# A two-layer hybrid trunk on one core: cached keys and values over four places, output blocks reordered, low weights in four pieces

## The chip, the core and the metric

The kernel runs on one core of one Trainium2 chip. The metric is device microseconds from start to end of one execution, the median of several. TensorE (PE) does the matrix products, VectorE (DVE) and ScalarE (ACT) take results out of PSUM, GpSimd (POOL) works from SBUF to SBUF, and SyncE (SP) issues most of the DMAs. Each engine works through its own list of instructions in order; semaphores are all that ties the lists together.

## The reference, cut to what matters

A prompt (1 x 1024 tokens) and a sample group (8 sequences of 4 tokens, 8192 past positions each) go through the same two layers with model width 1024. Layer 0 is a convolution module beside a dilated sliding-window attention, layer 1 a short gated convolution beside a chunked spatial gate; behind each mixer comes a SwiGLU of 2816. All is float32.

```python
def _dilated_attn_sample(q, k_ext, v_ext, d, rel_bias_table, grp):
    idx = Wb + np.arange(S)[:, None] - steps[None, :] * d      # 129 positions, stride 1, 4 or 16
    s = jnp.einsum('nshd,nskhd->nhsk', q, k_ext[:, idx_c]) * (Dh ** -0.5) + bias
    lse = jax.nn.logsumexp(s, axis=-1)
    o = jnp.einsum('nhsk,nskhd->nshd', jnp.exp(s - lse[..., None]), v_ext[:, idx_c])
...
out = jnp.concatenate([a, attn], axis=-1) @ P['e_w_out'][e]    # a: 256 channels, attn: 256
x = x + mod[:, 2] * out
h = _rmsnorm(x, P['norm_ffn_g'][layer]) * (1 + mod[:, 4]) + mod[:, 3]
gu = h @ P['ffn_w_gate_up'][layer]
```

For each of the 8 sequences the sample attention reads the keys and the values of its three groups from the caches, 9 tiles of 128 rows of 256 floats: 1152 KB for one set of keys, the same for one set of values.

## The kernel before

**Order.** `make_plan` writes one list of items (`Item`), and every engine's block walks through that list and emits its own part of each item. What stands earlier in the list is earlier on every engine. `mixed` and `among` spread one list of items evenly among another. SyncE alone walks through a list shifted by `ahead`: the stores of the prompt's keys and values of a group (`store_tokens`) come 16 items after their place.

**Dense products.** Weights come in units of 1 MB: SyncE loads a unit into one of three slots (`w_raw`), ScalarE rounds it to a high half (`split_hi`, L1061), and GpSimd subtracts to get the low half, in the place of the raw weights (`split_lo`, L2106). A product is high x high, high x low and low x high. PE waits on `w_lo_done`. A unit's split is emitted with the item of the unit before it. Results go to two PSUM places of three banks in turn (`big`); VectorE or ScalarE frees one (`big_free`) before PE writes it again.

**Around the sample attention.** The attention of the prompt's third group (`attention(2)`: scores, transpose, values, store, 16 steps) is mixed with the sample group's keys. For each sequence `b` five pieces of keys are transposed (`s_kt`, L2664; VectorE evacuates the even ones, ScalarE the odd ones), and three score products (`s_qk`, L2675) use them with `q_own`, which VectorE builds in the item `sample_in` (L1955, L1956). In the same stretch `ln_mid` (L1399, L1574) makes the two halves of the convolution's output, whose place on VectorE is free when the prompt's stores (`k_stored`) have landed. The keys lie in `cache`, two places; `load_cache` (L947 to L949) loads a set into a place when the set before it there has been used (`last_keys`), three DMAs each.

After the scores come the softmax (`s_soft`), the first unit of the output projection (`down_a`, eight blocks of 128 rows, `down_part`; VectorE evacuates each, L1567), the transposed weights `pT` (`s_pt`, L1409 on ScalarE, L1989 to L1993 on VectorE), the values (`s_pv`, L2712, 9 products a set) in pairs, each followed by `s_rows` and a block. Four blocks come before `s_pt`, four after the pairs. The values have three places. `comb` (L2000 to L2020) mixes the prompt's three groups on VectorE; `s_out`, `combine` and `mid_lo` (L2033) make the second half of the mixer's output, which `bound` needs: the last unit of the output projection with the next norm.

**Norm.** `bound` runs residual, norm and split in three turns of columns. For a turn VectorE makes `nt` (L1514), ScalarE `h_hi` (L1111, L1113, L1115), VectorE and GpSimd the even and odd `h_lo` (L1540, L2127), and PE takes products as they are made (`project_as_made`, L2342). Ahead of the third turn's lows GpSimd splits a unit: on GpSimd `lows(it, 1, ...)`, `split_lo(it.of.unit + 2)`, `lows(it, 2, ...)`. The third turn's VectorE part is `scaled_and_low(it, 2)`.

**Memory.** `cache` and the transposed keys lie where the first layer's `h_hi` was, `cache_v` over the transposed keys; `w_raw` slots 0 and 1 stand idle while the sample attention runs.

Of the kernel before, what the change touches and what calls it, by code (L numbers as in the profile page):

```python
# [172 lines left out]


# [6 lines left out]
def make_plan():  # L181
# [171 lines left out]
    mixed(last[:3], [])  # L353
    items.append(Item("sample_in"))
# [29 lines left out]
    def down_pieces(weights, col, **kw):  # L384

        made = []

        def piece(m):
            def place():
                if not made:  # L390
                    made.append(Item("down", weights=weights, col=col, unit=take("unit"), big=take("big", 8), **kw))
                items.append(Item("down_part", of=made[0], m=m, begins=m == 0, ends=m == KT - 1))
            return place

        return [piece(m) for m in range(KT)]

    down_a = down_pieces("e_w_out", 0, layer=0, gate=2, src="mid", slot=0, ready=1)
    for place in down_a[:4]:
        place()
# [12 lines left out]
    items.append(Item("combine", big=take("big", 2)))  # L412
    into_norm("e_w_out", 1, (0, 1), layer=0, gate=2, src="mid", slot=1, ready=2)
# [73 lines left out]
def build_trunk(nc: bass.Bass, A: dict, O: dict):  # L487
# [105 lines left out]
    cache_v = at("cache_v", R_HH + 18432, [P, 9, 256])  # L593
    o_sum = at("o_sum", R_V, [P, 4, 512])
# [46 lines left out]
    with ExitStack() as ctx:  # L641
# [70 lines left out]
        cache_loaded = [sem(f"cache_loaded{s}") for s in range(3)]  # L712
# [35 lines left out]
        for it in dense_items:  # L748
            unit_end[it.unit] = (big_ready, it.big + (2 + it.skip if it.kind == "project" else 8))
# [122 lines left out]
        def cached(c):  # L872

            slot = cache_at(c)[0]
            return cache_v if slot == 2 else cache[:, slot]
# [30 lines left out]
        def _(sp):  # L906
# [25 lines left out]
            def load_cache(c):  # L932

                kv, b = divmod(c, NB)
                if c == 0:
                    sp.wait_ge(big_ready, by_role["q", 2].big + 2)
                elif 2 <= c < NB + 2:
                    sp.wait_ge(misc_ready, last_keys[c - 2].misc + 1)
                elif c == NB + 2:
                    sp.wait_ge(big_ready, score_item.big + 1)  # L940
                elif c > NB + 2 and b % 2:
                    sp.wait_ge(v_used, (b - 3) // 2 + 1)
                elif c > NB + 2:
                    sp.wait_ge(misc_ready, values_of[b - 3].misc + 1)
                rows = [A[f"cache_b_kv{g}"][0, b, :, kv].rearrange("w h e -> w (h e)") for g in range(3)]
                to, loaded = cached(c), cache_loaded[cache_at(c)[0]]
                sp.dma_start(to[:, 0, :], rows[0]).then_inc(loaded, 16)  # L947
                sp.dma_start(to[:, 1:5, :], rows[1].rearrange("(j s) e -> j s e", s=4)).then_inc(loaded, 16)
                sp.dma_start(to[:, 5:9, :], rows[2].rearrange("(j s) e -> j s e", s=16)[:, 0:NS, :]).then_inc(loaded, 16)  # L949
# [46 lines left out]
            for it in ahead():  # L996
# [6 lines left out]
                elif it.kind == "tokens_store":  # L1003
                    store_tokens(it.of.g)
                elif it.kind == "ada":
                    order = ada_units.index(it)
                    if order < 2:
                        sp.wait_ge(x_loaded[(4, 7)[order]], 16)
                    elif order < 8:
                        raw_landed(ada_units[order - 2].raw)  # L1010
                    if it.raw.slot >= 4:
                        sp.wait_ge(x_turned, 2 * (it.raw.slot - 4) + 2)
                        sp.wait_ge(x_squared, 2 * (it.raw.slot - 4) + 2)
                    layer, cb = divmod(it.k, 24)
                    load_raw(it.raw, as_project, columns(A["ada_w"][layer], cb))
                elif it.kind in ("project", "down") or it.begins:
                    load_unit((it.of or it).unit + 1)
                elif it.kind == "sample_in":
                    load_cache(0)
                    load_cache(1)  # L1020
                elif it.kind == "s_kt" and it.c == 4:
                    load_cache(it.b + 2)
                elif it.kind == "s_soft":
                    load_cache(NB + 2)
                elif it.kind == "s_pv" and it.b + 3 < NB:
                    load_cache(NB + it.b + 3)
# [27 lines left out]
        def _(act):  # L1054
# [170 lines left out]
            for it in plan:  # L1225
# [102 lines left out]
                elif it.kind == "down_part":  # L1328
                    if it.begins and it.of.unit + 1 in unit_end:
# [762 lines left out]
        def _(pool):  # L2092
# [9 lines left out]
            def split_lo(u):  # L2102
# [3 lines left out]
                pool.tensor_tensor(w_lo[raw_of[u].slot], w_raw[raw_of[u].slot], w_hi[u % 2].bitcast(F32), ALU.subtract)\  # L2106
                    .then_inc(w_lo_done, 1)
                splits[0] = u + 1
# [28 lines left out]
            for it in plan:  # L2137
# [47 lines left out]
                elif it.kind == "bound":  # L2185
                    if it.of.unit + 1 in unit_end:
                        split_lo(it.of.unit + 1)
                    if it.role == "norm":
# [4 lines left out]
                        split_lo(it.of.unit + 2)  # L2193
                        lows(it, 2, (1, 3, 5, 7))
# [9 lines left out]
                elif it.kind == "down_part":  # L2204
                    if it.begins and it.of.unit + 1 in unit_end:
# [64 lines left out]
        def _(pe):  # L2270
# [22 lines left out]
            def project(u, t):  # L2293
                pe.wait_ge(w_lo_done, u + 1)
# [4 lines left out]
            def project_part(it, m, k):  # L2299

                if m == 0 and k == 0:
                    pe.wait_ge(w_lo_done, it.unit + 1)
# [3 lines left out]
            def first_products(it):  # L2306
# [3 lines left out]
                if it.which == "high":  # L2310
                    if it.k == 0:
                        pe.wait_ge(w_lo_done, u + 1)
# [20 lines left out]
            def project_as_made(u, t, it):  # L2333

                n = it.n
                pe.wait_ge(w_lo_done, u + 1)
# [37 lines left out]
            def down_blocks(it, x_hi, x_lo):  # L2374

                u, t = it.of.unit, it.of.big
                pe.wait_ge(w_lo_done, u + 1)
# [54 lines left out]
            def down(u, t, x_hi, x_lo, only=None):  # L2432
                if only in (None, 0):
                    pe.wait_ge(w_lo_done, u + 1)
# [12 lines left out]
            for it in plan:  # L2447
# [211 lines left out]
                elif it.kind == "s_kt":  # L2659
# [3 lines left out]
                    for j, (tile, a) in enumerate(KEY_PARTS[it.c]):  # L2663
                        mm = pe.transpose(misc(it.misc)[:, j * P:j * P + P], cached(it.b)[:, tile, a * P:a * P + P], ident)  # L2664
# [38 lines left out]
                elif it.kind == "s_pv":  # L2703
# [7 lines left out]
                    for t in range(9):  # L2711
                        mm = pe.matmul(misc(it.misc)[32 * (t % 4):32 * (t % 4) + 32, 256 * (b % 2):256 * (b % 2) + 256],  # L2712
                                       pT[:, t, b // 2:P:4],
                                       cached(c)[:, t, :], start=(t < 4), stop=(t >= 5), skip_group_check=True)
# [96 lines left out]
```

## Time and profile before

| | |
|---|---|
| median of 3 runs | 2604.43 us (2603.75 to 2606.38) |
| the profiled execution | 2611.14 us, its span 2609.3 us |
| TensorE busy | 2513.5 us (96%), mean granted clock 0.985 |
| VectorE, ScalarE, GpSimd busy | 914.0 (35%), 585.7 (22%), 510.6 us (20%) |
| chain that ended last | PE 73%, DVE 3%, ACT 2%, DMA 1%, issue 1% |
| `w_lo` on GpSimd | 93 instructions, 4639 ns mean |
| HBM | 228.04 MB read, 62.54 MB written, 111 GB/s over the span |

Two different executions stand in the table: the runs are timed without a profile, the span and all rows come from one profiled execution. Times in rows are microseconds from the start of its span. A row of the timeline has start, length, engine, line, operation, output and inputs with their shapes and a count; in brackets is how long the engine stood idle before it and what ended that. `q` behind an engine's name is its sequencer, which issues a DMA. An engine that is idle but not on the chain costs nothing.

### The profile page before, as it was taken

Reading aid. Unit: us, or ns where it says so; the run is one execution under the profiler, and the core shown is the slowest. Engines: PE = TensorE matmul, PEld = TensorE weight load, DVE = VectorE, ACT = ScalarE, POOL = GpSimd, SP = SyncE. Lnnn points to the kernel's source line nnn. Section 1 sums busy time; section 2 is a strip of 40 time slices with the busy share of each in tenths; the row PEclk is TensorE's granted clock in tenths of the full one; section 3 lists DMA queues with packets and bytes.
Section 4 is the critical chain, followed back from the end, with each engine's and each line's share of the span. In section 5 each row is a group of like instructions: output and inputs, shape, how many; then the busy total and the mean of one; then the engine's idle time right before and its main releaser. Section 6 shows DMA issues by size and latency. Waiting matters only on the chain.

```text
span 2609.3 us, 36572 instructions
## 1 busy us (share of the span) xinstructions
PE 2513.5 (96%) x16279; PEld 2393.7 (92%) x16279; DVE 914.0 (35%) x1679; ACT 585.7 (22%) x901; POOL 510.6 (20%) x209
## 2 busy tenths in 40 slices
PE   7999899889999999999999999999999999999998
PEld 6987778568999999999999899988999999999998
DVE  4366552556022222211224512546122222222226
ACT  5112223415111111111112411144211111111113
POOL 3210010103211221211211322122212221122210
PEclk8999999999999999999999999999999999999999
DMA  9322322770221222221221579311101111011101
GB/s 314 141 63 89 120 87 76 266 246 17 81 81 50 96 81 65 81 97 49 82 97 49 185 269 302 106 34 33 49 33 49 49 49 49 33 49 49 49 33 67
DMA packets 163963, 249.10 MB, mean 95 GB/s; under 512 B 6164, under 2 KB 150825, under 8 KB 162526
## 3 DMA queue, kind: packets, MB, share of 16 engines
q1 hardware_dynamic: 150762, 179.29, 20.9%
q0 software_dynamic: 4784, 63.31, 7.0%
q10 hardware_dynamic: 8260, 4.15, 0.6%
q8 instruction: 129, 2.11, 0.3%
q14 instruction: 28, 0.23, 0.0%
HBM read 228.04 MB, written 62.54 MB: 111 GB/s over the span
## 4 chain that ended last, share of the span: by engine, by line
PE 73%; DVE 3%; ACT 2%; DMA 1%; issue 1%; SPq 0%; ACTq 0%; DVEq 0%
PE ps L2286 66%; PE ps L2385 3%; PE ps L2520 1%; PE ps L2342 1%; DVE h_lo L1540 1%; DVE x L1475 1%; DMA w_raw<-in_e_w_out 0%; PE ps L2408 0%; ACT h_hi L1111 0%; PE ps L2712 0%; ACT nt L1113 0%; DVE nt L1514 0%; PE ps L2528 0%; ACT w_hi L1061 0%; ACT h_hi L1115 0%
## 5 line engine op out<-in xcount | busy, mean ns | idle before, releaser
L2106 POOL TENSOR_TENSOR w_lo<-w_raw,w_hi 128x2048 fp32r<-128x2048 f32 x93 | 431.4, 4639 | 1756.4 <-ACT w_hi L1061 1748.0
L2286 PE MATMUL ps<-h_hi,w_hi 128*128 128x352 f32 x2976 | 658.9, 330 | 6.1 <-ACT tmp L1066 3.0
L2286 PE MATMUL ps<-h_hi,w_lo 128*128 128x352 f32 x2976 | 644.3, 324 | 0.0
L2286 PE MATMUL ps<-h_lo,w_hi 128*128 128x352 f32 x2976 | 643.9, 325 | 0.0
L2286 PEld LDWEIGHTS ps<-h_hi,w_hi 128*128 128x128 f32 x2976 | 504.1, 190 | 26.6 <-issue 23.7
L2286 PEld LDWEIGHTS ps<-h_hi,w_lo 128*128 128x128 f32 x2976 | 513.2, 189 | 0.0
L2286 PEld LDWEIGHTS ps<-h_lo,w_hi 128*128 128x128 f32 x2976 | 508.7, 189 | 0.0
L1567 DVE SCALAR_TENSOR_TENSOR x<-ps,mod,x 128x704 f32<-128x704 f32 (+1 forms) x384 | 270.6, 746 | 285.9 <-PE ps L2286 285.9
L1616 DVE TENSOR_TENSOR tmp<-ps,tmp 128x1056 f32<-128x1056 f32 x44 | 55.3, 1258 | 722.7 <-PE ps L2286 722.7
L1061 ACT ACTIVATE w_hi<-w_raw 128x2048 fp32r<-128x2048 f32 x92 | 175.8, 1911 | 497.9 <-PE ps L2286 396.9
L2286 PE MATMUL ps<-mid_hi,w_hi 128*128 128x352 f32 x1104 | 240.5, 326 | 2.2 <-DVE acc_s L1568 1.6
L2286 PE MATMUL ps<-mid_hi,w_lo 128*128 128x352 f32 x1104 | 237.9, 323 | 0.0
L2286 PE MATMUL ps<-mid_lo,w_hi 128*128 128x352 f32 x1104 | 237.7, 323 | 0.0
L2286 PEld LDWEIGHTS ps<-mid_hi,w_hi 128*128 128x128 f32 x1104 | 187.4, 189 | 8.6 <-issue 6.8
L2286 PEld LDWEIGHTS ps<-mid_hi,w_lo 128*128 128x128 f32 x1104 | 189.6, 188 | 0.0
L2286 PEld LDWEIGHTS ps<-mid_lo,w_hi 128*128 128x128 f32 x1104 | 187.4, 188 | 0.0
L1066 ACT ACTIVATE tmp<-ps 128x1056 f32<-128x1056 f32 x52 | 54.4, 1052 | 447.3 <-PE ps L2286 436.8
L1171 ACT ACTIVATE mid_hi<-tmp 128x1056 fp32r<-128x1056 f32 x44 | 47.9, 1088 | 426.8 <-DVE tmp L1616 426.8
L1745 DVE TENSOR_TENSOR mod<-ps,vecs 128x18 f32<-128x18 f32 x48 | 8.4, 174 | 253.0 <-PE ps L2528 252.9
L1845 DVE SCALAR_TENSOR_TENSOR conv_a<-ext_p,vecs,conv_a 128x1024 f32<-128x1024 f32 x60 | 89.1, 1485 | 0.0
L1574 DVE TENSOR_TENSOR mid_lo<-tmp,mid_hi 128x1056 fp32r<-128x1056 f32 x50 | 62.3, 1254 | 0.6 <-ACT mid_hi L1399 0.6
L1475 DVE SCALAR_TENSOR_TENSOR x<-ps,mod,x 128x352 f32<-128x352 f32 (+1 forms) x96 | 51.0, 566 | 28.1 <-PE ps L2385 27.8
(337 smaller groups left out, 1996.2 us busy)
## 6 DMA issues: line engine op xcount, KB each, us to landing
w_raw<-in_ada_w SPq DMA_DIRECT2D x48, 1024.0 KB, 6.6
w_raw<-in_ffn_w_gate_up SPq DMA_DIRECT2D x44, 1024.0 KB, 5.1
out_kv_sample<-in_cache_b_kv POOLq DMA_DIRECT2D x8, 4088.0 KB, 19.6
w_raw<-in_ffn_w_down SPq DMA_DIRECT2D x22, 1024.0 KB, 4.9
cache<-in_cache_b_kv SPq DMA_DIRECT2D x28, 512.0 KB, 5.8
w_raw<-in_e_w_in SPq DMA_DIRECT2D x11, 1024.0 KB, 5.6
w_raw<-in_o_w_in SPq DMA_DIRECT2D x10, 1024.0 KB, 10.1
out_kv_sample<-in_cache_b_kv POOLq DMA_DIRECT2D x8, 1016.0 KB, 6.4
```

Source lines behind the costliest of these rows:

```text
L1061: act.activation(w_hi[u % 2], w_raw[r.slot], ACT.Copy).then_inc(w_hi_done, 1)
L1066: return act.activation(blocks(dst), big(t)[:, :, 0:BLK], func, **kw).then_inc(big_free[t % 2], 1)
L1171: act.activation(mid_hi[:, it.j % 2, m, :], tmp[:, m, :], ACT.Copy).then_inc(hid_hi, 1)
L1475: ins = dve.scalar_tensor_tensor(x[:, m, c], big(t)[:, bank, 0:c.stop - c.start], mod[:, 6 * d.layer + d.gate, m, 0:1], x[:, m, c], ALU.mu ...
L1540: dve.scalar_tensor_tensor(h_lo[:, k, c], nt[:, k, c], mod[:, 6 * it.layer + 3 * it.which, k, 0:1], h_hi[:, k, c].bitcast(F32), ALU.add, A ...
L1567: dve.scalar_tensor_tensor(dst, src, g, dst, ALU.mult, ALU.add)
L1574: return dve.tensor_tensor(dst, src, hi.bitcast(F32), ALU.subtract)
L1616: dve.tensor_tensor(blocks(tmp[:, m, :]), T[:, :, 0:BLK], blocks(tmp[:, m, :]), ALU.mult)\
L1845: ins = dve.scalar_tensor_tensor(dst, src, w, dst, ALU.mult, ALU.add)
L2106: pool.tensor_tensor(w_lo[raw_of[u].slot], w_raw[raw_of[u].slot], w_hi[u % 2].bitcast(F32), ALU.subtract)\
L2286: mm = pe.matmul(big(t)[:, b, 0:BLK], wt, xt[:, k, b * BLK:b * BLK + BLK], start=(k == 0 and n == 0), stop=(k == K - 1 and n == 2))
L2385: mm = pe.matmul(big(t + i)[:, bank, 0:BLK], halves[s][:, k, m * P:m * P + P], xt[:, k, c], start=(k == 0 and n == 0), stop=(k == 1 and n ...
```

## The change

- Sets of keys use four places: `cache`'s two, and two made of `w_raw` slots 0 and 1 (eight tiles each) with a small tile each in `R_T`. Values use `cache`'s two, `cache_v` and the place in `w_raw` slot 1.
- A new item `cache_in`, at the start of `attention(2)`, loads set 0 (into the first new place, when the adaLN unit in slot 0 has been used and group 1's scores are done). The first three key pieces stand among the first three attention items, ahead of `sample_in`; sets 1 to 3 are loaded at `sample_in`, set 3 behind a wait for set 1's landing. The ring of PSUM banks starts before these items. A later set is asked for when the set four before it (keys) or four before it (values) has been used.
- The load of the last unit of the output projection waits for the fifth sequence's last key piece, that of the next unit for the fourth even sequence's values, since those places hold keys and values.
- Three output blocks stand before `s_pt`, four after the pairs, the eighth after `combine`; the split of the next unit comes with the fourth block instead of the first.
- `w_lo` is made in four instructions of 512 columns everywhere; in a norm's third turn GpSimd's lows stand between the pieces.

```diff
+LO_PIECES = 4
...
     last = attention(2)
-    mixed(last[:3], [])
-    items.append(Item("sample_in"))
+    items.append(Item("cache_in"))
     scores = take("big")
     items.append(Item("ring", n=1, big=scores, misc=n["misc"]))
...
-    sample = []
-    for b in range(NB):
-        sample += [keys(b, 0)] + ([scored(b - 1, 2)] if b else [])
+    mixed(last[:3], [keys(0, 0), keys(0, 1), keys(0, 2)])
+    items.append(Item("sample_in"))
+    sample = [scored(0, 0), keys(0, 3), scored(0, 1), keys(0, 4)]
+    for b in range(1, NB):
+        sample += [keys(b, 0), scored(b - 1, 2)]
         sample += [keys(b, 1), scored(b, 0), keys(b, 2), keys(b, 3), scored(b, 1), keys(b, 4)]
...
+    down_a = Item("down", weights="e_w_out", col=0, layer=0, gate=2, src="mid", slot=0, ready=1, unit=take("unit"),
+                  big=take("big", 7), skip=2)
+    def down_piece(m):
+        items.append(Item("down_part", of=down_a, m=m, begins=m == 0, splits=m == 3))
+    for m in range(3):
+        down_piece(m)
     items.append(Item("s_pt", misc=take("misc", 3)))
...
         if b % 2:
             items.append(Item("s_rows", b=b // 2, misc=values[-1]))
-            down_a[4 + b // 2]()
+            down_piece(3 + b // 2)
...
     items.append(Item("combine", big=take("big", 2)))
+    after = replace(down_a, big=take("big") - 7)
+    items.append(Item("down_part", of=after, m=7))
...
+    cache_w = [at(f"cache_w{s}", R_W + 8192 * s, [P, 8, 256]) for s in range(2)]
+    cache_t = [at(f"cache_t{s}", R_T + 12544 + 1024 * s, [P, 256]) for s in range(2)]
...
-            return (c % 2, c // 2 + 1) if b < 0 else (b % 3, b // 3 + (1 if b % 3 == 2 else 5))
+            return ((3, 0, 1, 4)[c % 4], c // 4 + 1) if b < 0 else ((0, 1, 4, 2)[b % 4], b // 4 + (1 if b % 4 == 3 else 3))
...
                 if c == 0:
+                    sp.wait_ge(*key_raw.before)
+                    sp.wait_ge(sc_max, 32)
+                elif c == 1:
                     sp.wait_ge(big_ready, by_role["q", 2].big + 2)
-                elif 2 <= c < NB + 2:
-                    sp.wait_ge(misc_ready, last_keys[c - 2].misc + 1)
-                elif c == NB + 2:
+                elif c == 3:
+                    sp.wait_ge(cache_loaded[cache_at(1)[0]], 48)
+                elif 4 <= c < NB:
+                    sp.wait_ge(misc_ready, last_keys[c - 4].misc + 1)
+                elif NB <= c < NB + 3:
+                    sp.wait_ge(misc_ready, last_keys[c - 3].misc + 1)
+                elif c == NB + 3:
                     sp.wait_ge(big_ready, score_item.big + 1)
...
+                if raw_of[u] is key_raw:
+                    sp.wait_ge(misc_ready, last_keys[4].misc + 1)
+                elif raw_of[u] is both_raw:
+                    sp.wait_ge(v_used, 4)
...
                 elif it.kind == "down_part":
-                    if it.begins and it.of.unit + 1 in unit_end:
+                    if it.splits:
                         split_hi(it.of.unit + 1)
...
+            def lo_piece(u, q):
+                c = slice(2048 // LO_PIECES * q, 2048 // LO_PIECES * (q + 1))
+                pool.tensor_tensor(w_lo[raw_of[u].slot][:, c], w_raw[raw_of[u].slot][:, c], w_hi[u % 2].bitcast(F32)[:, c], ALU.subtract)\
                     .then_inc(w_lo_done, 1)
...
                         lows(it, 1, (1, 3, 5, 7))
-                        split_lo(it.of.unit + 2)
-                        lows(it, 2, (1, 3, 5, 7))
+                        pool.wait_ge(w_hi_done, it.of.unit + 3)
+                        for q, ks in enumerate(((), (1,), (3,), (5, 7))):
+                            lo_piece(it.of.unit + 2, q)
+                            lows(it, 2, ks)
...
-                pe.wait_ge(w_lo_done, u + 1)
+                pe.wait_ge(w_lo_done, LO_PIECES * (u + 1))
```

## Rows read from the trace of the kernel before

**Rows 1.** Timeline of TensorE in the sample attention: start, length, what [idle before it]
```profile
462.97 0.69 PE L2664 MATMUL ps<-ident_sb,cache 128*128 128x128 f32 x2 [0.80 <-DMA cache<-in_cache_b_kv]
...
483.10 0.44 PE L2664 MATMUL ps<-ident_sb,cache 128*128 128x128 f32 x2 [2.83 <-DMA cache<-in_cache_b_kv]
...
485.69 0.43 PE L2675 MATMUL ps<-kT,q_own 128*32 128x128 f32 x8
...
491.80 0.44 PE L2664 MATMUL ps<-ident_sb,cache 128*128 128x128 f32 x2 [1.51 <-DMA cache<-in_cache_b_kv]
```

**Rows 2.** Timeline of TensorE around the value products
```profile
549.61 0.33 PE L2697 MATMUL ps<-ident_sb,p_s 128*128 128x128 f32 x1 [4.16 <-ACT pT L1409]
...
551.32 5.31 PE L2712 MATMUL ps<-cache,pT 128*32 128x256 f32 x36 [0.99 <-DVE pT_n L1993]
...
574.62 1.51 PE L2712 MATMUL ps<-cache,pT 128*32 128x256 f32 x18 [0.93 <-DMA cache<-in_cache_b_kv]
...
590.43 0.43 PE L2385 MATMUL ps<-mid_hi,w_hi 128*128 128x352 f32 x1 [2.59 <-DVE mid_lo L1574]
```

**Rows 3.** Timeline of GpSimd in the first norm's third turn
```profile
637.36 4.63 POOL L2106 TENSOR_TENSOR w_lo<-w_raw,w_hi 128x2048 fp32r<-128x2048 f32 x1 [0.86 <-ACT w_hi L1061]
641.94 1.24 POOL L2127 TENSOR_TENSOR h_lo<-nt,h_hi 128x352 fp32r<-128x352 f32 x1
...
644.59 0.94 POOL L2127 TENSOR_TENSOR h_lo<-nt,h_hi 128x352 fp32r<-128x352 f32 x1 [0.50 <-ACT h_hi L1115]
```

**Rows 4.** Timeline of VectorE in the first and the third norm
```profile
637.79 4.58 DVE L1540 SCALAR_TENSOR_TENSOR h_lo<-nt,mod,h_hi 128x352 fp32r<-128x352 f32 x1 [0.44 <-ACT h_hi L1111]
...
1825.68 4.57 DVE L1540 SCALAR_TENSOR_TENSOR h_lo<-nt,mod,h_hi 128x352 fp32r<-128x352 f32 x1 [0.45 <-ACT h_hi L1111]
```

**Rows 5.** Timeline of SyncE's queue at the start of the sample attention
```profile
456.52 0.35 SPq L947 DMA_DIRECT2D cache<-in_cache_b_kv  x1
...
460.86 1.85 SPq L966 DMA_DIRECT2D out_kv_prompt<-k_rows  x2
```

**Rows 6.** Timeline of VectorE in the sample attention
```profile
463.98 0.25 DVE L1956 COPY q_rows<-q_new 128x96 f32<-128x96 f32 x1
...
478.44 2.43 DVE L1574 TENSOR_TENSOR mid_lo<-tmp,mid_hi 128x1056 fp32r<-128x1056 f32 x2 [0.58 <-ACT mid_hi L1399]
```

**Rows 7.** Windows: busy (count) of PE, PEld, DVE, ACT, POOL, granted clock, DMA share, GB/s
```profile
461.50:471.50 10.00, 9.20 (x50) 6.76 (x50) 5.96 (x31) 3.91 (x16) 0.53 (x1) 0.50 1.02 366
335.00:341.00 6.00, 5.44 (x20) 4.75 (x21) 3.21 (x8) 0.39 (x1) 0.00 (x0) 0.50 0.00 0
```

**Rows 8.** Timeline of ScalarE ahead of the values
```profile
547.16 1.91 ACT L1061 ACTIVATE w_hi<-w_raw 128x2048 fp32r<-128x2048 f32 x1 [11.25 <-DMA w_raw<-in_e_w_out]
548.97 0.58 ACT L1409 ACTIVATE pT<-ps 128x512 f32<-128x512 f32 x1
```

**Rows 9.** Chain of waits: start, length, what (an output block, then `s_out`)
```profile
576.13 3.11 PE ps L2286 x18
...
580.72 3.71 PE ps L2730 x32
```

**Rows 10.** Timeline of VectorE from `comb` to `mid_lo`
```profile
567.15 0.18 DVE L2000 TENSOR_TENSOR comb<-nat 128x32 f32<-128x32 f32 x1
...
581.31 1.40 DVE L1567 SCALAR_TENSOR_TENSOR x<-ps,mod,x 128x704 f32<-128x704 f32 x2
...
587.44 1.23 DVE L2033 TENSOR_TENSOR mid_lo<-ps,mid_hi 128x1024 fp32r<-128x1024 f32 x1 [2.08 <-ACT mid_hi L1423]
```

**Rows 11.** Windows of L2342 alone (PE, PEld), second and third turn
```profile
633.33:638.73 5.40, 5.40 (x32) 5.29 (x33) 1.00 0.01 3
641.29:648.37 7.08, 5.93 (x35) 5.06 (x34) 1.00 0.00 0
```

**Rows 12.** Timeline of VectorE, then of TensorE, in the convolution
```profile
330.80 4.25 DVE L1845 SCALAR_TENSOR_TENSOR conv_a<-ext_p,vecs,conv_a 128x1024 f32<-128x1024 f32 x1
...
335.56 1.23 PE L2626 MATMUL ps<-qk_fm 64*128 64x256 f32 x4 [2.49 <-DVE o_rows L1908]
```

More of the change, by code:

```diff
@@ L20 @@
 from contextlib import ExitStack
-from dataclasses import dataclass
+from dataclasses import dataclass, replace
 import numpy as np
@@ L382, in make_plan @@
     items.append(Item("s_soft", big=scores, misc=n["misc"] - 1))
[L384 to L399, printed above, removed]
+    down_a = Item("down", weights="e_w_out", col=0, layer=0, gate=2, src="mid", slot=0, ready=1, unit=take("unit"),
[4 more added lines that the diff above has]
+        down_piece(m)
     items.append(Item("s_pt", misc=take("misc", 3)))
@@ L711, in build_trunk @@
         smp_loaded, sel_loaded, qw_zero, qw_made = sem("smp_loaded"), sem("sel_loaded"), sem("qw_zero"), sem("qw_made")
-        cache_loaded = [sem(f"cache_loaded{s}") for s in range(3)]
+        cache_loaded = [sem(f"cache_loaded{s}") for s in range(5)]
         new_half, s_qked = sem("new_half"), sem("s_qked")
@@ L748, in build_trunk @@
         for it in dense_items:
-            unit_end[it.unit] = (big_ready, it.big + (2 + it.skip if it.kind == "project" else 8))
+            unit_end[it.unit] = (big_ready, it.big + (2 if it.kind == "project" else 8) + it.skip)
         LO_DVE = (0, 2, 4, 6)
@@ L869, in cache_at, with cached @@
             b = c - NB
-            return (c % 2, c // 2 + 1) if b < 0 else (b % 3, b // 3 + (1 if b % 3 == 2 else 5))
-        def cached(c):
+            return ((3, 0, 1, 4)[c % 4], c // 4 + 1) if b < 0 else ((0, 1, 4, 2)[b % 4], b // 4 + (1 if b % 4 == 3 else 3))
+        def cached(c, t0, t1):
             slot = cache_at(c)[0]
-            return cache_v if slot == 2 else cache[:, slot]
+            if slot < 3:
+                return (cache_v if slot == 2 else cache[:, slot])[:, t0:t1, :]
+            return cache_t[slot - 3].unsqueeze(1) if t0 == 0 else cache_w[slot - 3][:, t0 - 1:t1 - 1, :]
+        down_first = next(it.of for it in plan if it.kind == "down_part" and it.begins)
+        key_raw, both_raw = raw_of[down_first.unit + 1], raw_of[down_first.unit + 2]
+        assert (key_raw.slot, both_raw.slot) == (0, 1) and raw_of[down_first.unit].slot == 2
         DOWN_M = (4, 5, 6, 7, 0, 1, 2, 3)
@@ L1017, in _ @@
                     load_unit((it.of or it).unit + 1)
+                elif it.kind == "cache_in":
+                    load_cache(0)
                 elif it.kind == "sample_in":
[L1019 to L1022, printed above, removed]
+                    for c in range(1, 4):
+                        load_cache(c)
+                elif it.kind == "s_kt" and it.c == 4 and it.b != 4:
+                    load_cache(it.b + 4 if it.b < 4 else it.b + 3)
                 elif it.kind == "s_soft":
-                    load_cache(NB + 2)
-                elif it.kind == "s_pv" and it.b + 3 < NB:
-                    load_cache(NB + it.b + 3)
+                    load_cache(NB + 3)
+                elif it.kind == "s_pv" and it.b < 4:
+                    load_cache(NB + it.b + 4)
             for i, n in enumerate(OUT_ORDER[:8]):
@@ L2104, in split_lo @@
                 pool.wait_ge(w_hi_done, u + 1)
-                pool.tensor_tensor(w_lo[raw_of[u].slot], w_raw[raw_of[u].slot], w_hi[u % 2].bitcast(F32), ALU.subtract)\
+                for q in range(LO_PIECES):
+                    lo_piece(u, q)
+            def lo_piece(u, q):
+                c = slice(2048 // LO_PIECES * q, 2048 // LO_PIECES * (q + 1))
+                pool.tensor_tensor(w_lo[raw_of[u].slot][:, c], w_raw[raw_of[u].slot][:, c], w_hi[u % 2].bitcast(F32)[:, c], ALU.subtract)\
                     .then_inc(w_lo_done, 1)
-                splits[0] = u + 1
+                splits[0] = LO_PIECES * u + q + 1
             def splits_done():
@@ L2204, in _ @@
                 elif it.kind == "down_part":
-                    if it.begins and it.of.unit + 1 in unit_end:
+                    if it.splits:
                         split_lo(it.of.unit + 1)
@@ L2311, in first_products @@
                     if it.k == 0:
[L2312 removed]
+                        pe.wait_ge(w_lo_done, LO_PIECES * (u + 1))
                         pe.wait_ge(x_copied, 8)
@@ L2713, in _ @@
                                        pT[:, t, b // 2:P:4],
-                                       cached(c)[:, t, :], start=(t < 4), stop=(t >= 5), skip_group_check=True)
+                                       cached(c, t, t + 1)[:, 0, :], start=(t < 4), stop=(t >= 5), skip_group_check=True)
                     mm.then_inc(misc_ready if b % 2 else v_used, 1)
```

26 lines of the change are left out of this document (13 added, 13 removed).

## The prediction

> **What bounds the kernel now.** I read the chain of waits first: nearly all of it is TensorE (PE), so time can only come out of stretches where PE stands still or runs slowly. TensorE's rows, looked through for idle time, show three such stretches that the change touches. In the sample attention (457 to 530 us) PE waits for cached keys: 0.80, 2.83 and 1.51 [rows 1]. Around the value products (530 to 590) it waits 4.16 for ScalarE's copy of the transposed weights, 0.99 and 0.93 after that, and 2.59 before the next norm [rows 2]. In the norms and in the convolution it waits for a VectorE that is itself held: an `h_lo` of 352 columns lasts 4.58 at 637.79 and ends with the `w_lo` that GpSimd runs beside it [rows 3, 4]. Everywhere else PE is full, and there a fourfold split of `w_lo` lies beside matmuls and costs nothing.
>
> **Part A, the keys (457 to 530).** Before, SyncE issues sets 0 and 1 from 456.52 and stores the prompt's rows from 460.86 [rows 5]; PE starts set 0 at 462.97 [rows 1], 6.5 after its issue. Changed, set 0 is asked for ahead of the last projection products (its two waits are for work that PE has left behind by then) and is there when attention starts. Three terms follow.
> - The start. Three key pieces now stand before `sample_in`. VectorE copies two of them (0.4 + 0.7) before it builds `q_own`, which then ends not at 464.23 [rows 6] but near 465.9; the first scores product, now right behind the third piece, waits for it from about 462. By 465.9 PE has done two key pieces more and two attention steps less than before: some 0.2 lost. The 0.80 is not won.
> - The stores. SyncE now issues sets 1 and 2 at 456.5, stops until set 1 has landed (462.97, as set 0 did before), issues set 3, and only then the stores: about 464.7 in place of 460.86. Set 4 and all later loads queue behind them. VectorE's `ln_mid` waits for the stores; it ran at 478.44 before [rows 6], so they had landed. The DMAs are full there, share 1.02 at 366 GB/s [rows 7], so the 3.8 are not made up: the stores land near 482, `ln_mid` (2.4) ends at 484.4, VectorE copies the key piece that PE needs (0.4), and PE goes on at 484.9. Before, it was at that product at 485.69 [rows 1]. So of the 2.83 only 0.8 is won, less 0.9 for two attention steps that are still to come.
> - Later sets. With four places a set is asked for over 10 us before its use; the 1.51 goes.
>
> Part A wins 0.8 - 0.9 + 1.5 - 0.2 = 1.2. Bounds: 5.1 won (all three key waits) and 4 lost (stores another 5 late).
>
> The Trainium skill (SBUF — State Buffer, Summary: rules for kernel authors) says to reckon HBM traffic at about 358 GB/s. The 366 GB/s of the row agrees; by the rule the 1.18 MB set that goes ahead of the stores shifts them by 3.3 us (an estimate), and the term would be 0.5 better.
>
> **Part B, the values (530 to 590).** Before, ScalarE must split the next weights at 547.16, after 11.25 idle until their load landed, and only then copies `pT` at 548.97 [rows 8]; the first value product starts at 551.32 [rows 2]. Changed, that split comes behind the first pair of values, and three output blocks instead of four stand ahead.
> - PE stands from 549.61 - 4.16 = 545.45 [rows 2]; before that lie eight transposes (about 1.0) and block four (3.1 [rows 9]), so block three ends at 541.4 either way. Four transposes and ScalarE's 0.58: 542.6. VectorE first evacuates block three (1.4 [rows 10] and a small one), then copies the other parts of `pT` (1.5): 544.8. The values start 6.5 earlier, of which 3.1 is the block moved: 3.4 won.
> - The values lasted from 551.32 to 576.13 + 3.11 = 579.24 [rows 2, 9]: 27.9 for eight sets and four blocks, and it is eight and four again. The first two sets took 5.31, where one set takes 1.51 [rows 2]: 2.3 lost to a slow TensorE after the idle. Waits for late sets, 0.93 [rows 2] and a smaller one, are 1.4. Set 3 is now asked for when the scores end, the others a pair ahead of use: 12 us of PE work against some 6 of loading. I take both, 3.7 won: the values end at 569.0. The idle left ahead of them, 1.5, I judge too short to bring the slow clock; if it does, 2.3 stays lost.
> - VectorE's chain is next. `comb` runs from 567.15 to 581.31, 14.2 [rows 10]. Changed, it starts behind block four's evacuation, 544.8 + 12.2 + 1.6 = 558.6, and ends at 572.8; the first slot for `combine` is free 1.6 later, at 574.4, the second at 575.9. PE's `s_out` takes from 579.24 to 580.72 + 3.71 = 584.43 [rows 9], 5.2, and ends at 574.2. The two meet within 0.2, the second slot 1.5 later at worst.
> - The last block behind `combine`: its slot is free when the first `mid_lo` is done, 587.44 + 1.23 [rows 10], 4.3 after `s_out`'s end. It fills the 2.59 of idle before 590.43 [rows 2] and runs past it: the norm starts 7.4 (full speed) to 9.5 (half) after `s_out`, where it was 6.0. I take 8.5: 574.4 + 8.5 = 582.9 against 590.43.
>
> Part B wins 7.5. Bounds 4 (slow clock again, VectorE 1.5 late) and 9.5.
>
> **Part C, `w_lo` in pieces, in the norms.** VectorE's `h_lo` is held from 637.79 to GpSimd's end; the last of the three norms has it at 1825.68 [rows 3, 4]. The third turn takes 7.08 where the second takes 5.40 for the same products [rows 11]: 1.68 each. Does VectorE get in between two pieces? GpSimd's next `h_lo` at 641.94 took 1.24, the one at 644.59 took 0.94 [rows 3]: it waited 0.3 for VectorE, so yes. A piece costs (4.63 - 0.94) x 512/1696 + 0.18 = 1.3. VectorE then ends its first `h_lo` at 639.1 in place of 642.37, its last `nt` near 641.8; ScalarE ends the last `h_hi` near 643.3, before PE asks at 644 to 646. GpSimd ends its last low at 647.9, 0.8 before its use. 3 x 1.68 = 5.0 won. Bounds 0 and 5.8.
>
> The Trainium skill (SBUF — State Buffer, Who interferes with whom) says that a VectorE instruction with two SBUF inputs and a GpSimd instruction that reads SBUF exclude each other for their whole length, and that the order of issue decides which waits. The 4.58 agrees; by that rule an `h_lo` waiting since 637.79 goes ahead of a piece issued later, the same 5.0, and it speaks against rival 3.
>
> **Part D, the same in the convolution.** `conv_a` took 4.25 at 330.80, and PE then waited 2.49 [rows 12]; a like place is at 276. With pieces, two of them still pass before VectorE's next two such instructions are done: 1.05 earlier, twice, 2.1 won. Bounds 0 and 9: idle here is followed by a granted clock of 0.50, the 1.2 GHz level, at 335 to 341 as at 461 to 471 [rows 7]; if some 6.8 us of that go in both places, 3.4 more each.
>
> **Sum.** 1.2 + 7.5 + 5.0 + 2.1 = 15.8 off the profiled execution's 2611.14 (span 2609.3 and 1.8 around it). That run lies 6.7 above the median of the runs, 2604.43; off the median, 2588.6.
>
> **The rivals.**
> 1. The late stores and VectorE's chain take more: A loses 4, B wins 4. For it: the chains meet within 1.5 on paper, and the DMAs are full. Against: neither is a wait before. 4 + 5 + 2.1 - 4 = 7.1 won: 2597.
> 2. Less idle also keeps TensorE at its fast level, twice in the convolution (6.8) and once more in the attention (2): 24.6 won, 2580. For it: each slow stretch stands behind idle. Against: 1.4 of the 2.49 stays.
> 3. Slower: GpSimd's pieces follow each other without letting VectorE in. It decides when the second piece starts before the `h_lo` that waits. Four pieces and four lows, 4 x 1.3 + 4 x 0.94 = 9.0, hold VectorE to 646.4 in place of 642.4, three times: 12 lost, and 2.3 each for a slow TensorE behind such idle, 6.9; D wins nothing. 18.9 - 1.2 - 7.5 = 10.2 slower: 2615. Against: the row at 641.94.
> 4. The change doesn't do what it says: the pieces bring VectorE nothing, and the values stay tied to `comb`. B 4, A 1.2: 2599.
>
> **How the numbers follow.** Forecast 45 in 100 (2583 to 2594 by its own bounds), rival 1 20, rival 2 20, rival 4 11, rival 3 4. A measurement of this kernel can't tell 0.2% (5.2 us, 2599.2 to 2609.6) from no change. The forecast and rivals 1 and 2 lie below that, 85; rival 4 at its edge counts as the same, 11; slower 4. The range, 2577 to 2599, leaves out rival 3, half of rival 4 and the ends of 1 and 2.
>
> **What will show it.** Right: no key wait over 0.5; `ln_mid` on VectorE near 482, behind the stores; ScalarE's `pT` copy straight behind the transposes, values from about 545 to 570; the norm's third turn at 5.4; `h_lo` under 2 us beside `w_lo`. Wrong: an `h_lo` over 4 us in a norm (C), PE waiting more than 3 for `comb` (B), `ln_mid` later than 487 (A).

## The result, and the profile after

The changed kernel takes 2587.22 us (median of 6 runs, 2586.41 to 2590.01); the kernel before, with more runs, 2607.12 (6 runs, 2603.75 to 2610.51). The ratio is 0.9927, 95% interval 0.9914 to 0.9939: 19.9 us faster. A second set of six runs on another occasion gave 2586.04 against 2608.21, ratio 0.9911 (0.9888 to 0.9933). The profiled execution of the changed kernel took 2587.36, span 2585.5. Two executions of the experiments below, one of `split_first` and one of `both`, ran in a slower state of the chip (granted clock 0.905 and 0.749, at least 45 us longer) and are left out.

TensorE's products are the same 16279 in both traces, so the two can be laid over each other by counting them. The lead of the changed kernel is how much earlier the same product starts in its trace. It wanders by up to 1 us either way ahead of 271 us, where it stands at 0.55. From there it grows in five places: in the convolution (270 to 367 us), around the values, and 1.9 to 2.0 us in each of the three norms. It falls by 0.89 in the sample attention, and elsewhere it moves by 0.2 at most. I call the stretches D, A, B and C as in the prediction. First the windows of the kernel before, from one counted product to another: D, A, B. Columns as in [rows 7].

```profile
271.45:367.51 96.06, 82.89 (x530) 71.43 (x529) 51.84 (x92) 24.79 (x74) 10.98 (x5) 0.88 0.33 104
449.19:530.83 81.64, 69.58 (x574) 46.43 (x574) 38.79 (x122) 35.70 (x107) 7.71 (x9) 0.94 0.74 252
530.83:600.78 69.95, 59.21 (x414) 50.36 (x415) 38.23 (x78) 14.17 (x22) 10.01 (x3) 0.90 0.57 186
```

The same windows of the changed kernel:

```profile
270.90:357.71 86.81, 75.69 (x530) 65.62 (x529) 50.45 (x92) 24.82 (x74) 14.17 (x11) 0.96 0.37 116
439.25:521.78 82.53, 71.43 (x575) 46.11 (x574) 37.94 (x122) 35.74 (x107) 7.71 (x9) 0.90 0.77 258
521.78:582.99 61.21, 57.07 (x415) 51.15 (x415) 38.31 (x78) 14.27 (x22) 10.98 (x9) 0.92 0.58 194
```

D is 9.25 shorter, A 0.89 longer, B 8.74 shorter. In D the mean granted clock went from 0.88 to 0.96: most of its 9.25 is TensorE at 2.4 GHz where it was at 1.2 (its busy time falls from 82.89 to 75.69 for the same products).

**A.** Timeline of TensorE of the changed kernel, what answers to [rows 1]: the key waits are gone and three waits for VectorE stand there.

```profile
456.00 0.65 PE L2702 MATMUL ps<-kT,q_own 128*32 128x128 f32 x8 [3.12 <-DVE q_rows L1975]
...
470.31 1.07 PE L2702 MATMUL ps<-kT,q_own 128*32 128x512 f32 x8 [0.98 <-DVE kT L1981]
...
475.27 0.66 PE L2702 MATMUL ps<-kT,q_own 128*32 128x128 f32 x8 [2.70 <-DVE kT L1981]
```

Behind the last of them TensorE falls to its slow level once more (windows, columns as in [rows 7]):

```profile
473.00:478.00 5.00, 2.73 (x18) 1.79 (x19) 3.37 (x7) 0.41 (x1) 1.71 (x3) 0.63 1.02 343
478.00:482.00 4.00, 4.00 (x23) 2.01 (x22) 0.90 (x4) 1.63 (x6) 0.00 (x0) 0.60 1.11 377
```

VectorE there, against [rows 6]: `ln_mid` stands 2.29 for the prompt's stores, and the key copy that PE wants comes behind it.

```profile
472.45 2.43 DVE L1593 TENSOR_TENSOR mid_lo<-tmp,mid_hi 128x1056 fp32r<-128x1056 f32 x2 [2.29 <-DMA out_kv_prompt<-v_tok]
474.80 0.42 DVE L1981 COPY kT<-ps 128x256 f32<-128x256 f32 x1
```

SyncE's queue, against [rows 5]: set 3 (`cache_t`) goes out at 453.21, the stores behind it at 455.77.

```profile
449.38 0.62 SPq L962 DMA_DIRECT2D cache<-in_cache_b_kv  x1
453.21 0.34 SPq L960 DMA_DIRECT2D cache_t<-in_cache_b_kv  x1
...
455.77 5.78 SPq L979 DMA_DIRECT2D out_kv_prompt<-k_rows  x2
```

**B.** ScalarE of the changed kernel, against [rows 8]: the `pT` copy at once, the split 6 us later, behind the first pair of values.

```profile
533.33 0.60 ACT L1428 ACTIVATE pT<-ps 128x512 f32<-128x512 f32 x1 [6.48 <-PE ps L2724]
538.67 0.60 ACT L1431 ACTIVATE o_sum<-ps 128x512 f32<-128x512 f32 x1 [4.75 <-PE ps L2739]
539.17 1.90 ACT L1080 ACTIVATE w_hi<-w_raw 128x2048 fp32r<-128x2048 f32 x1
```

Its chain of waits, against [rows 2, 9]: two sets in 2.78 where the first two took 5.31, no wait among the values. Before the last block stands VectorE's `mid_lo`, for which PE waits 0.78; that block takes 4.79 where the others take 3.10.

```profile
535.86 2.78 PE ps L2739 x36
...
556.13 3.10 PE ps L2313 x18
...
568.44 1.24 DVE mid_lo L2052
569.68 0.04 issue
569.72 4.79 PE ps L2313 x18
```

From the end of `s_out` to the norm the granted clock is 0.57 (window):

```profile
565.43:574.51 9.08, 8.30 (x37) 7.90 (x37) 4.11 (x11) 3.77 (x6) 0.00 (x0) 0.57 0.00 0
```

**C.** VectorE in the first norm's third turn, against [rows 4]: the `h_lo` that took 4.58 takes 1.24.

```profile
619.99 1.24 DVE L1559 SCALAR_TENSOR_TENSOR h_lo<-nt,mod,h_hi 128x352 fp32r<-128x352 f32 x1 [0.44 <-ACT h_hi L1130]
```

Windows of L2369 alone, second and third turn, against [rows 11]: 5.13, where it was 7.08, and PE busy in all of it.

```profile
615.52:620.92 5.40, 5.39 (x32) 5.29 (x33) 1.00 0.02 3
623.48:628.61 5.13, 5.13 (x35) 5.13 (x33) 1.00 0.00 0
```

**D.** VectorE, then TensorE, against [rows 12]: the longest `conv_a` is 2.16, and the wait of 2.49 is 1.15.

```profile
279.67 2.16 DVE L1864 SCALAR_TENSOR_TENSOR conv_a<-ext_p,vecs,conv_a 128x1024 f32<-128x1024 f32 x1
...
329.81 0.70 PE L2653 MATMUL ps<-qk_fm 64*128 64x256 f32 x4 [1.15 <-DVE o_rows L1927]
```

What it cost stands in the groups by line: GpSimd's low weights, 431.4 us in 93 instructions before, are 489.1 in 372. That lies beside TensorE, and the lead shows no loss from it.

```profile
L2131 POOL TENSOR_TENSOR w_lo<-w_raw,w_hi 128x512 fp32r<-128x512 f32 x372 | 489.1, 1344 | 1692.5 <-ACT w_hi L1080 1684.1 <-DVE diag L1665 8.4
```

### The profile page after: what moved, and what is told of

The parts are those of the page before. It is cut to its first block, busy times and chain, and to the rows that moved or that the text cites. A ratio compares the mean times of both kernels' runs of the same rounds, so it can differ in the third digit from the quotient of the medians.

```text
span 2585.5 us, 36854 instructions
## 1 busy us (share of the span) xinstructions
PE 2498.1 (97%) x16279; PEld 2383.1 (92%) x16279; DVE 897.5 (35%) x1679; ACT 584.9 (23%) x901; POOL 568.5 (22%) x488
## 4 chain that ended last, share of the span: by engine, by line
PE 76%; DVE 2%; ACT 1%; issue 1%; ACTq 0%; DVEq 0%
PE ps L2313 67%; PE ps L2412 3%; PE ps L2369 2%; PE ps L2547 1%; DVE x L1494 1%; PE ps L2435 0%; PE ps L2739 0%; PE ps L2555 0%; PE ps L2583 0%; DVE nt L1533 0%; DVE tmp L1938 0%; PE ps L2757 0%; PE ps L2702 0%; ACT ln_t L1228 0%; DVE x L1586 0%
## 5 line engine op out<-in xcount | busy, mean ns | idle before, releaser
L2131 POOL TENSOR_TENSOR w_lo<-w_raw,w_hi 128x512 fp32r<-128x512 f32 x372 | 489.1, 1344 | 1692.5 <-ACT w_hi L1080 1684.1
L1864 DVE SCALAR_TENSOR_TENSOR conv_a<-ext_p,vecs,conv_a 128x1024 f32<-128x1024 f32 x60 | 81.0, 1351 | 0.0
```

Source lines behind the costliest of these rows:

```text
L1864: ins = dve.scalar_tensor_tensor(dst, src, w, dst, ALU.mult, ALU.add)
L2131: pool.tensor_tensor(w_lo[raw_of[u].slot][:, c], w_raw[raw_of[u].slot][:, c], w_hi[u % 2].bitcast(F32)[:, c], ALU.subtract)\
```

## The experiments

Each run left a profile, cut at the same counted products. The table has these stretches (us); C is the sum of the three norms, each counted from the first to the last product of `project_as_made`. "Pieces" are the four pieces of `w_lo`.

| kernel | D | A | B | C |
|---|---|---|---|---|
| before | 96.06 | 81.64 | 69.95 | 91.89 |
| before_again | 96.29 | 79.97 | 71.31 | 91.96 |
| norm_only | 92.10 | 83.46 | 71.15 | 86.12 |
| conv_only | 85.56 | 82.95 | 71.04 | 92.15 |
| norm_plain | 88.73 | 79.85 | 69.24 | 86.04 |
| memory_only | 91.51 | 81.25 | 61.01 | 92.02 |
| old_blocks | 88.51 | 81.01 | 67.62 | 85.95 |
| split_first | 87.26 | 81.85 | 67.64 | 86.00 |
| after | 86.81 | 82.53 | 61.21 | 85.99 |
| after_again | 88.73 | 80.97 | 63.17 | 86.10 |
| stores_first | 86.42 | 77.60 | 62.75 | 85.95 |
| ln_later | 86.78 | 81.71 | 61.13 | 86.15 |
| own_halves | 85.77 | 85.91 | 61.00 | 86.13 |
| both | 88.83 | 78.03 | 62.62 | 86.09 |

**The parts alone.** Pieces everywhere but in the norms, on the kernel before:

```diff
+            def split_lo(u, pieces=4):      # 4 instructions; the norms' third turn calls it with 1
```

> The kernel before, with only one edit: low weights in four pieces everywhere but in the norms' third turns (there still one instruction). Theory 1 (the pieces shorten VectorE's conv_a at two places, 2.3 us of waits, and the idle that goes also takes away the slow stretches of TensorE behind it, some 7 us): 9 us faster than the kernel before, and no granted clock of 0.5 between 276 and 360 us but the one near 320. Theory 2 (the slow stretches fall where they fall in one execution and not in another): 2 us faster, slow stretches there as in the kernel before.

2601.45 against 2608.21, ratio 0.9973 (0.9961 to 0.9985): 7 us, 4 to 10 by the interval, nearer to the 9 of theory 1 than to the 2 of theory 2. D is 85.56 with a granted clock of 0.98; the one slow spell left lies near 320, as theory 1 has it.

Pieces in the norms' third turns only, with GpSimd's lows between them:

```diff
-                        split_lo(it.of.unit + 2)
-                        lows(it, 2, (1, 3, 5, 7))
+                        pool.wait_ge(w_hi_done, it.of.unit + 3)
+                        for q, ks in enumerate(((), (1,), (3,), (5, 7))):
+                            lo_piece(it.of.unit + 2, q, 4)
+                            lows(it, 2, ks)
```

> The kernel before, with only one edit: in the norms' third turns the low weights come in four pieces with GpSimd's lows between them, elsewhere in one. Theory 1 (VectorE gets in between two pieces): each of the three third turns 1.9 to 2.0 us shorter, 5.9 us faster in all. Theory 2 (the third turn gains from the rest of the change, the waits in front of it): under 2 us.

2600.09, ratio 0.9977 (0.9960 to 0.9993): 6 us. C is 5.8 shorter, three times 1.9 to 2.0: theory 1. But D, whose code is that of before, is 92.10 here:

```profile
266.78:358.88 92.10, 78.81 (x530) 69.18 (x529) 52.04 (x92) 24.92 (x74) 10.98 (x5) 0.93 0.36 109
```

The same instructions (GpSimd's 5, not 11), and 4 us less, at a granted clock of 0.93 in place of 0.88. So part of what D shows between two profiles is one execution against another.

The rest of the change without the pieces:

```diff
-LO_PIECES = 4
+LO_PIECES = 1
...
-                        for q, ks in enumerate(((), (1,), (3,), (5, 7))):
+                        for q, ks in enumerate(((1, 3, 5, 7),)):
```

> The changed kernel with the low weights in one instruction again: cached sets over four places and the block order alone. Theory 1 (parts are independent): 8 us faster than the kernel before, of it 0.8 lost in the sample attention and 8.7 won around the values; slow stretches between 283 and 359 us as before. Theory 2 (the pieces are needed there too, since GpSimd's low weights hold VectorE around the values): under 5 us.

2595.52, ratio 0.9952 (0.9933 to 0.9972): 12.5 us, more than the 8 expected, with an interval from 7 to 17. B is 61.01: the pieces have no part in it. Theory 2 falls. D, expected as before, is 91.51.

> The changed kernel itself, to have its time on the same chip beside its parts, and a second profile. If the parts are independent, its gain is the sum of the three (theory 1: 9 + 5.9 + 8 = 23). If the slow stretches of TensorE are a matter of chance, they lie elsewhere in this profile than in the first (theory 2: 16 to 18 us faster).

22.2 us faster (ratio above); the three parts' ratios add up to 7 + 6 + 12.5 = 25.5, within their intervals: nearer to theory 1. D is 88.73, granted 0.94, against 86.81 and 0.96 in the first profile of this kernel.

> The kernel before itself, for a second profile of the same program. Theory 1 (the slow stretches in the convolution belong to the long conv_a): granted clock 0.5 again near 284 and 335. Theory 2 (they are a matter of chance): other places, and the time between 270 and 367 us differs by 3 us or more from the first profile, with the same waits.

2608.32. D is as in the first profile of this kernel, theory 1 for this one:

```profile
269.27:365.56 96.29, 83.02 (x530) 71.54 (x529) 51.93 (x92) 24.87 (x74) 10.97 (x5) 0.88 0.33 105
```

With norm_only and memory_only the code without pieces has given 96.06, 96.29, 92.10 and 91.51, mean 94.0; ten profiles with pieces gave 85.56 to 88.83, mean 87.3. The two sets don't touch. The pieces are worth 6.7 in D on average, which the 7 of conv_only's timed runs bears out; a single pair says anything from 2.7 to 10.7.

Cut finer, the clock isn't mere chance. The prediction's rival 2 has two places in D: the products from 283.89, behind waits of 0.81 and 0.91, and those behind the 2.49. The same products at both places, before, then in norm_only, then in the changed kernel:

```profile
283.89:291.01 7.12, 7.12 (x35) 4.82 (x36) 1.70 (x4) 0.38 (x1) 0.00 (x0) 0.52 0.44 141
335.56:342.02 6.46, 6.46 (x24) 5.74 (x25) 2.65 (x5) 1.41 (x5) 0.00 (x0) 0.51 0.00 0
```

```profile
279.27:283.32 4.05, 4.05 (x34) 2.89 (x35) 1.70 (x4) 0.38 (x1) 0.00 (x0) 1.00 0.30 74
326.87:333.35 6.48, 6.48 (x24) 5.76 (x25) 2.65 (x5) 1.43 (x5) 0.00 (x0) 0.51 0.00 0
```

```profile
282.34:286.41 4.07, 4.07 (x34) 2.91 (x35) 1.70 (x4) 0.38 (x1) 0.00 (x0) 1.00 0.29 76
329.81:333.79 3.98, 3.77 (x24) 3.18 (x24) 3.42 (x5) 0.77 (x2) 0.83 (x1) 1.00 0.02 4
```

Without pieces the slow spell is there at both places in before and before_again, at the second alone in norm_only, at the first alone in memory_only (0.53, then 1.00): six times of eight. With pieces it is at neither place in any of the ten profiles. Each costs 2.5 to 3.1.

**The norms' order on GpSimd.**

```diff
+            def split_lo(u, pieces=4):
...
                         split_lo(it.of.unit + 2)            # as before, now four pieces
                         lows(it, 2, (1, 3, 5, 7))           # as before, behind them
```

> The kernel before with the low weights in four pieces everywhere, but GpSimd's lows of the third turn behind all four pieces, not between them. Theory 1 (what helps is that VectorE gets in between two pieces): the third turn as in the changed kernel within 0.5 us, 5.2 to 5.6. Theory 2 (the lows between the pieces are what helps; behind all four they come too late): 6 us or more, since four pieces that alternate with VectorE end later than one instruction did.

C is 86.04 against 86.12 with the lows between the pieces. VectorE gets in between pieces that GpSimd issues back to back (its `h_lo` takes 1.25 there); in this one profile, with its three norms, the interleaved lows are worth nothing. One run, 2593.30.

**Around the values.**

```diff
-                  big=take("big", 7), skip=2)
+                  big=take("big", 8))
...
-    for m in range(3):
+    for m in range(4):                       # splits=m == 0; no block behind the combine
```

> The changed kernel with the output blocks as in the kernel before: four ahead of the transposed weights, four behind the pairs, none behind the combine, and the split of the next weights with the first block. Theory 1 (the block order and the place of the split make part B): the stretch from the start of the first block to the next norm is 7 us longer than in the changed kernel, so some 15 us faster than the kernel before instead of 22. Theory 2 (the sets of values asked for earlier make part B, the order is worth little): no more than 3 us of part B is lost, 19 or more us faster than the kernel before. In both the waits for late values, 0.93 and a smaller one, don't come back.

2595.57, ratio 0.9950 (0.9935 to 0.9966): 13 us. B is 67.62, and no wait for late values is back: theory 1, with 5.8 in place of 7.

```diff
-        items.append(Item("down_part", of=down_a, m=m, begins=m == 0, splits=m == 3))
+        items.append(Item("down_part", of=down_a, m=m, begins=m == 0, splits=m == 0))
```

> The changed kernel with one edit: the split of the next weights comes with the first output block again, in front of ScalarE's copy of the transposed weights. Theory 1 (the split in front of the copy was the 4.16 us wait): the wait for that copy comes back at 3 to 5 us, TensorE then runs its first values at the slow level (2 us more), and the stretch to the next norm is 4 to 6 us longer than in the changed kernel, unless VectorE's chain for the combine hides 1 or 2 of them. Theory 2 (the load lands earlier now that keys lie in that slot and it is asked for at another time, so the split is done before the copy): under 1 us.

2595.82, ratio 0.9953 (0.9931 to 0.9974). Theory 1. B is 67.64, the same as with all of the old order. So in the new order the place of the split is worth 67.6 - 61.8 (mean of the seven with the new order) = 5.8, and with the split in front the order of the blocks is worth nothing. The old order of blocks with the late split was not run. ScalarE of split_first: the `pT` copy is behind a split that waited 9.39 for its load.

```profile
536.96 1.91 ACT L1080 ACTIVATE w_hi<-w_raw 128x2048 fp32r<-128x2048 f32 x1 [9.39 <-DMA w_raw<-in_e_w_out]
538.77 0.58 ACT L1428 ACTIVATE pT<-ps 128x512 f32<-128x512 f32 x1
```

TensorE of the same kernel: the wait, and two sets of values at the slow level, 5.31 for 2.78. All seven profiles with the split in front, those of the old order among them, have 4.72 to 5.31 here, all seven with the late split 2.78.

```profile
539.40 0.47 PE L2724 MATMUL ps<-ident_sb,p_s 128*128 128x128 f32 x1 [4.83 <-ACT pT L1428]
...
541.51 5.31 PE L2739 MATMUL ps<-cache,pT 128*32 128x256 f32 x36 [0.99 <-DVE pT_n L2012]
```

The five profiles with the old order and two places give B 70.5 on average; the sets over four places make 67.6 of it, 2.9.

**What is left in A.** Five profiles with the old places have A at 81.6 on average, the five changed ones that leave A as it is 81.5. So A won nothing; four edits ask why.

```diff
-                    for c in range(1, 4):
+                    for c in range(1, 3):
                         load_cache(c)
...
                     store_tokens(it.of.g)
+                    if it.of.g == 2:
+                        load_cache(3)
```

> The changed kernel with one edit: SyncE issues the prompt's stores of the third group ahead of set 3 of the keys (set 3 with its wait for set 1 behind them). Theory 1 (the stores were late only because SyncE stood at that wait): they are issued near 4 us earlier, VectorE's ln_mid doesn't hold the next key copy any more, TensorE's wait of 2.5 to 3.6 us for it goes, part A is 2 to 3 us shorter than in the changed kernel. Theory 2 (the stores' time is the DMA queues' time, whatever the order): ln_mid moves by under 1 us, part A the same or, with set 3 later, longer.

2580.03 against 2605.12, ratio 0.9900 (0.9883 to 0.9917). A is 77.60, 3.9 less than the changed kernels' mean. SyncE of stores_first issues the stores at 452.23, 2.6 behind set 2's first DMA (7.5 in the changed kernel, 448.25 to 455.77):

```profile
449.66 0.51 SPq L960 DMA_DIRECT2D cache<-in_cache_b_kv  x1
...
452.23 1.65 SPq L979 DMA_DIRECT2D out_kv_prompt<-k_rows  x2
```

and its VectorE no longer waits at `ln_mid`:

```profile
471.60 2.42 DVE L1595 TENSOR_TENSOR mid_lo<-tmp,mid_hi 128x1056 fp32r<-128x1056 f32 x2
473.94 0.42 DVE L1983 COPY kT<-ps 128x256 f32<-128x256 f32 x1
```

Theory 1 holds, and A won more than its 2 to 3: with the wait of 2.5 to 3.6 (now 0.31) the slow spell behind it is gone too.

```profile
474.00:479.00 5.00, 4.69 (x43) 2.94 (x44) 2.64 (x9) 2.57 (x10) 1.72 (x3) 1.00 1.09 365
479.00:483.00 4.00, 4.00 (x39) 2.38 (x40) 2.32 (x8) 1.86 (x6) 0.00 (x0) 1.00 1.08 404
```

In all eight other profiles with the new places a wait of 2.5 to 7.0 for a key copy stands here, and a spell at the slow level behind it. The set that hastened the keys had delayed the stores, and VectorE behind them.

```diff
-    mixed(last[3:15] + [one("ln_mid"), one("sample_load")] + ...
+    mixed(last[3:20] + [one("ln_mid", n=0)] + last[20:23] + [one("ln_mid", n=1), one("sample_load")] + ...
```

> The changed kernel with one edit: ln_mid in two halves, five and eight attention items later on VectorE and ScalarE. Theory 1 (the 2.5 to 3.6 us wait is VectorE standing in front of the stores with key copies queued behind it): the wait goes, part A 2.5 to 3.6 us shorter; up to 2 more if the slow stretch behind it goes as well. Theory 2 (another wait ends just behind it, a key set or GpSimd's loads that wait for ln_mid): under 1 us.

2585.73, ratio 0.9919 (0.9904 to 0.9934); A is 81.71. Theory 2: I moved ScalarE's half of the item with VectorE's, and VectorE now waits for that.

```profile
474.73 1.26 DVE L1592 TENSOR_TENSOR mid_lo<-tmp,mid_hi 128x1056 fp32r<-128x1056 f32 x1 [1.99 <-ACT mid_hi L1417]
```

```diff
+    sample = [scored(0, 0), keys(0, 3), scored(0, 1), keys(0, 4), one("own_odd")]   # odd half of q_own
```

> The changed kernel with one edit: VectorE builds only the even sequences' half of q_own in front of the first scores product, the odd half behind the first sequence's key pieces. Theory 1 (the 3.1 to 3.45 us wait is VectorE building q_own): the wait falls by 1.6, the time of one half, and part A is 1.6 us shorter, or up to 2 with less slow clock behind it. Theory 2 (VectorE is the bound of these 20 us): the half comes back as waits for key copies, under 0.5.

2591.11, ratio 0.9938 (0.9924 to 0.9952); A is 85.91, 4.4 longer. Neither theory: the wait for `q_own` did fall from 3.12 to 1.60, and VectorE came to `ln_mid` sooner, stood 4.84 there for the same stores, and PE with it, 6.95, and then 9 us at a granted clock of 0.50:

```profile
470.88 1.94 PE L2703 MATMUL ps<-kT,q_own 128*32 128x512 f32 x8 [6.95 <-DVE kT L1981]
```

> The changed kernel with the two edits together, ln_mid in two later halves and q_own in two halves. Theory 1 (the two waits are what part A has left): part A 4 to 5 us shorter than in the changed kernel, 26 us faster than the kernel before, so faster than both. Theory 2 (VectorE or the DMA queues are the bound of part A): under 2 us of that is seen.

2581.28, ratio 0.9903 (0.9887 to 0.9919); A is 78.03, 3.5 less. Of the 4 to 5 expected most is there, and by the ratio 25 of the 26 us, though a wait of 2.88 for a key copy stays.

Of all versions stores_first has the lowest median and the shortest A, with `both` 1.3 us behind. Its interval meets that of the changed kernel (0.9888 to 0.9933 on its second occasion), so by the timed runs it is likely, not shown, to be the faster of the two.

## Why the prediction was right, and where not

2588.6 was forecast, 2587.2 came, but two errors cancel, and that the total is so near is luck. The gain forecast was 15.8; measured were 19.9 and 22.2, and the four parts below add up to some 21.4. The median it was taken from, 2604.43 of three runs, was low: larger sets of the same kernel gave 2605 to 2608.

**A, 1.2 forecast, 0.1 measured** (81.6 against 81.5, single profiles 79.9 to 83.5). The mechanism stood, each step to within 1.0. Taken to the clock of the trace before (9.94 added), `q_own` was done at 465.9 as forecast, the stores were issued at 465.7 (464.7 forecast), `ln_mid` ended at 484.8 (484.4), PE went on at 485.2 (484.9). Not in the sum: 0.98 for another key copy, and a second spell at the slow level behind the 2.70. The spell comes in every profile with that wait, and its length changes: A's granted clock was 0.90 in the first profile of this kernel, 0.94 in the second.

**B, 7.5 forecast, 8.7 measured** (means 70.5 and 61.8). With 9.05 added for the lead at the first block: values from 544.9 (544.8 forecast) to 568.3 (569.0), `comb`'s chain done at 572.4 (572.8), the norm's start 583.4 (582.9). The judgement that 1.5 of idle would bring no slow level held, 2.78 for two sets. From the end of `s_out` to the norm it was 8.9, where 8.5 was forecast: the slow spell that lay on the norm's first products, behind the 2.59, now lies on `combine` and the last block (4.79 for 3.10). The steps inside are shared out otherwise than I had it: of the 8.7, 5.8 come with the place of the split and 2.9 with the four places. What moving blocks three, four and eight adds to the late split, no run shows.

**C, 5.0 forecast, 5.95 measured** (means 92.00 and 86.05). VectorE gets in between pieces, as the row at 641.94 had said; the turn became 5.13, not 5.40. I had taken the second turn as the floor, which it is not. Rival 3 is out, at every place looked at.

The Trainium skill (SBUF — State Buffer, Who interferes with whom) has the issue order decide who waits. The 1.25 and 1.24 beside pieces issued back to back, in norm_plain and in the changed kernel, agree.

**D, 2.1 forecast, 6.7 measured: the step that was mis-sized.** The waits went as reckoned: 0.81 to nothing, 2.49 to 1.15 and 0.20. The rest, 4.6 on average, is the clock, for which I had put 6.8 into rival 2 at 20 in 100. So in D rival 2 happened: both slow spells go with the pieces, in all ten profiles. It comes to two thirds of its 6.8, since a spell costs less than 3.4 and two of the eight weren't there without pieces either. In A it did not happen: another spell came there. Mean granted clock in D: 0.88, 0.88, 0.93 and 0.93 without pieces, 0.92 to 0.98 with them; a further spell near 320 comes in all 14.

Rival 1 has not happened: in B TensorE has no idle time between `s_out` and the combine, so the two chains do meet. Rival 4 is out, by memory_only and conv_only.

## What to carry to other kernels

An instruction that holds up another engine for 4.6 us is worth cutting wherever something waits behind that engine, even at 13% more busy time, if its own engine has room. When a load is put ahead on a queue, look at what its wait now holds up behind it: here the stores, 3.9 us. And where TensorE falls to its lower clock level in some executions, judge an edit by several profiles of one stretch, not by one pair, and count the slow spells place by place: a shorter wait can take a spell away with it, as in D, and a new wait can bring one, as in A.

## What was not expected of the hardware

The code without pieces, with the same instructions and nearly the same waits, ran D at a granted clock of 0.88 twice and of 0.93 twice, 4 us apart. The stretch ahead of it, 4 to 271 us, was touched by no edit but the pieces and went from 262.4 to 268.7 us in the 14 profiles. The Trainium skill (TensorE: Matmul & The Clock Gate, Part 1) says that the number of products at the slow level when a kernel starts varies from run to run. The rows above show the same in the middle of one: behind the same wait the slow spell comes in one execution and not in another.

Issuing DMAs held SyncE itself: the four stores of `k_rows` and `v_tok` took it 9.8 us before (1.85 and 7.96), 9.8 in the changed kernel (5.78 and 3.98) and 10.4 in stores_first (1.65 and 8.73), where the key loads ahead of them take 0.34 to 0.76 each; what stands behind them in its queue waits as long.
